# One 1 MB stage of expert weights: fetched in three pieces on earlier signals, copied inside the first swish, with the token count behind it

## The reference

```python
def hier_moe(h, w_group, b_group, w_fine, b_fine, w_gate, w_up, w_down):
    x2 = h.reshape(n_tok, d)
    g_prob = softmax(x2 @ w_group + b_group)            # 4 groups, the best one is taken
    g_val, grp = lax.top_k(g_prob, 1)
    f_logits = x2 @ w_fine + b_fine                     # 8 experts in that group, the best two
    top_v, top_i = lax.top_k(f_in_group, MOE_TOPK)
    gates = g_val * softmax(top_v)
    ...
    def expert_block(args):                             # for every expert
        xb = x2[tok]
        hid = jax.nn.silu(xb @ w_gate[e]) * (xb @ w_up[e])
        return hid @ w_down[e]
```

## Time and profile before

| | |
|---|---|
| median of 3 runs | 1109.93 us (1109.8 to 1110.1) |
| the profiled execution's own time | 1110.2 us |
| its span, first to last instruction | 1108.4 us |
| PE busy | 903.1 us (81%) |
| DVE busy | 416.5 us (38%) |
| ACT busy | 243.8 us (22%) |
| POOL busy | 41.9 us (4%) |
| moved by DMA | 440.73 MB, mean 398 GB/s |
| mean granted TensorE clock | 0.910 |

### The profile page before, as it was taken

How to read it: one execution, slowest core, us unless ns; L and a number is a source line. 1 busy time by engine, 2 the same in 40 slices (tenths; PEclk the granted TensorE clock), 3 DMA queues, 4 the chain that set the end, 5 groups by cost and what they waited for, 6 DMA issues and landing times.

```text
span 1108.4 us, 21929 instructions
## 1 busy us (share of the span) xinstructions
PE 903.1 (81%) x9146; PEld 593.1 (54%) x9146; DVE 416.5 (38%) x1006; ACT 243.8 (22%) x622; POOL 41.9 (4%) x65
## 2 busy tenths in 40 slices
PE   9999989978685867677799998999676858585875
PEld 6877745645353535353488676656443525353532
DVE  6888433332222222222288665333221222222222
ACT  5567311100000000000265863111010000000012
POOL 0012200000000000000000312000000000000000
PEclk9999989989887888788999999999887978888899
DMA  9898999999999999999998668999999999999995
GB/s 353 251 402 334 358 410 429 427 429 429 429 428 428 429 427 429 429 429 428 408 386 345 233 270 356 427 427 429 427 430 429 427 428 430 427 428 430 429 426 234
DMA packets 56577, 440.73 MB, mean 398 GB/s; under 512 B 12113, under 2 KB 12625, under 8 KB 31058
## 3 DMA queue, kind: packets, MB, share of 16 engines
q1 hardware_dynamic: 56240, 440.02, 95.7%
q10 hardware_dynamic: 290, 0.07, 0.0%
HBM read 439.03 MB, written 1.05 MB: 397 GB/s over the span
## 4 chain that ended last, share of the span: by engine, by line
PE 49%; DMA 35%; SPq 5%; another core or an unknown queue 3%; DVE 3%; ACT 2%; issue 1%; POOL 0%; POOLq 0%; ACTq 0%; DVEq 0%
DMA ring<-in_w_expert_up 27%; PE banks L1138 14%; DMA ring<-in_w_expert_down 7%; PE banks L1166 6%; PE banks L1106 6%; PE banks L1179 3%; PE banks L1015 3%; PE banks L1019 3%; PE banks L1016 3%; SPq L524 2%; SPq L472 1%; PE banks L1232 1%; PE banks L1234 1%; PE banks L1233 1%
## 5 line engine op out<-in xcount | busy, mean ns | idle before, releaser
L1138 PE MATMUL banks<-ring,scratch 128*32 128x256 f32 x4096 | 287.2, 443 | 129.2 <-DMA ring<-in_w_expert_up 128.8
L1138 PEld LDWEIGHTS banks<-ring,scratch 128*32 128x32 f32 x4096 | 150.3, 127 | 260.2 <-issue 122.2
L1665 DVE TENSOR_SCALAR scratch<-scratch 128x128 f32<-128x128 f32 x64 | 14.5, 227 | 510.3 <-ACT scratch L779 507.6
L1166 PE MATMUL banks<-ring,xn 128*32 128x256 f32 x2048 | 137.0, 410 | 7.7 <-DMA ring<-in_w_expert_down 7.5
L778 ACT ACTIVATE scratch<-banks 128x128 f32<-128x128 f32 x64 | 17.8, 278 | 511.1 <-PE banks L1138 499.7
L1106 PEld LDWEIGHTS banks<-scratch,h 128*128 128x128 f32 x448 | 107.7, 334 | 5.8 <-issue 5.8
L1106 PE MATMUL banks<-scratch,h 128*128 128x128 f32 x448 | 110.4, 405 | 0.0
L1179 PE MATMUL banks<-xn 32*128 32x256 f32 x1024 | 74.8, 403 | 36.5 <-ACT xn L788 36.5
L1166 PEld LDWEIGHTS banks<-ring,xn 128*32 128x32 f32 x2048 | 63.6, 116 | 60.0 <-issue 23.1
L1179 PEld LDWEIGHTS banks<-xn 32*128 32x128 f32 x1024 | 50.3, 186 | 67.8 <-issue 67.7
L1440 DVE SCALAR_TENSOR_TENSOR split<-ring,gains,split 128x512 fp32r<-128x512 f32 x96 | 69.7, 765 | 24.1 <-ACT split L826 23.3
(11 more groups left out here) (177 smaller groups left out, 792.9 us busy)
## 6 DMA issues: line engine op xcount, KB each, us to landing
ring<-in_w_expert_gate SPq DMA_DIRECT2D x62, 2048.0 KB, 45.5
ring<-in_w_expert_up SPq DMA_DIRECT2D x61, 2048.0 KB, 48.8
ring<-in_w_expert_down SPq DMA_DIRECT2D x56, 2048.0 KB, 47.5
ring<-in_w_in_even SPq DMA_DIRECT2D x5, 2048.0 KB, 17.8
ring<-in_w_expert_down SPq DMA_DIRECT2D x10, 1024.0 KB, 10.0
ring<-in_w_in_odd SPq DMA_DIRECT2D x5, 2048.0 KB, 19.7
ring<-in_w_expert_up SPq DMA_DIRECT2D x6, 1024.0 KB, 11.0
ring<-in_w_out_even SPq DMA_DIRECT2D x2, 2048.0 KB, 9.0
```

The lines of the kernel that those rows point to most:

```text
L1138: last = pe.matmul(psum[6][32 * j:32 * j + 32, 0:2 * P].rearrange("p (a s) -> p a s", a=2), xT[:, c, SLOTS * k:SLOTS * k + SLOTS], ring[:, ...
L1166: last = pe.matmul(psum[4][32 * q:32 * q + 32, 0:QUARTER], hidT[k][:, 32 * j:32 * j + 32], ring[:, DOWN_AT[k], D * j + QUARTER * q:D * j + ...
```

## The change

SP fetches the stage in three pieces: columns 0 to 1023 (512 KB) after `placed` has its second signal of the layer, which PE sends behind the first `gather_first`; columns 1024 to 1535 and 1536 to 2047 (256 KB each) after the first and the second signal of `gathered`. On DVE, `count_rounds` is split in two. The gate shares stay where they were. `copy_stage` moves into `hidden` of expert 0, between the swish and the transpose, and the token count follows behind that transpose; the wait for POOL's gates follows it.

```diff
+STAGE_PIECES = (1024, 1536, 2048)
...
-                sp.wait_ge(gathered[l], 2)
-                sp.dma_start(stage, gate_rows[row][:, 0:512 * FIRST_PIECES[0]]).then_inc(stage_arrived, 16)
+                for begin, end in zip((0,) + STAGE_PIECES, STAGE_PIECES):
+                    if begin == 0:
+                        sp.wait_ge(placed, (T + 1) * l + T)
+                    else:
+                        sp.wait_ge(gathered[l], STAGE_PIECES.index(end))
+                    sp.dma_start(stage[:, begin:end], gate_rows[row][:, begin:end]).then_inc(stage_arrived, 16)
...
-                pool.wait_ge(stage_arrived, 16 * (l + 1))
+                pool.wait_ge(stage_arrived, 16 * len(STAGE_PIECES) * (l + 1))
...
-            def count_rounds(l, link):
+            def choice_shares(l, link):
 
                 dve.wait_ge(gexp_done, T * (l + 1))
                 by = gv[:, 8:10]
                 link(dve.scalar_tensor_tensor(out=by, in0=gv[:, 4:6], scalar=1.0, in1=gv[:, 2:4],
                                               op0=ALU.add, op1=ALU.mult))
                 dve.reciprocal(by, by).then_inc(first_gates, 1)
+
+            def count_tokens(l, link):
 
                 dve.wait_ge(placed, (T + 1) * (l + 1))
...
-                dve.wait_ge(stage_arrived, 16 * (l + 1))
+                dve.wait_ge(stage_arrived, 16 * len(STAGE_PIECES) * (l + 1))
...
                 dve.tensor_tensor(hb, eb, gb[:, P:2 * P], ALU.mult).then_inc(hid_ready[l], 1)
+                if first:
+                    copy_stage(l)
                 dve.wait_ge(hid_ready[l], e + 1)
...
-                count_rounds(l, route_link)
-                dve.wait_ge(gate_steps, GATE_STEPS * (l + 1))
-                copy_stage(l)
+                choice_shares(l, route_link)
                 for k in range(AHEAD):
                     hidden(l, k, k, first=(k == 0), links=0)
+                    if k == 0:
+                        count_tokens(l, route_link)
+                        dve.wait_ge(gate_steps, GATE_STEPS * (l + 1))
                     gate_slots(l, k, k, k, links=SILU_LINKS)
```

## The result

The changed kernel takes 1112.18 us (median of 15 runs, 1109.99 to 1115.46) where the kernel before takes 1109.80 (1107.95 to 1111.53): a ratio of 1.0025, with a 95% interval of 1.0017 to 1.0033. It is slower by 2.4 us between the medians and by 2.8 us by the ratio. My 1111.2 us, 1.3 over the kernel before, lay on the right side with half the size, and "within 0.2%", which I took for the likeliest outcome, was missed by a little; the time lies inside the 1109.9 to 1112.4 of my own case. The profiled execution has a span of 1111.0 us, 2.6 over that of before.

What follows compares the result with a forecast made beforehand. The transfer queue was taken to bound the loops, with PE mattering where it runs short. Later pairs added 0.35 us in layer 0 and 0.95 in layer 1, together +1.3: 1111.2 us, eight-in-ten range 1108.3 to 1113.5.

Steps and rivals of the forecast that it cites:

- within 0.2%: Whole kernel: the time can't be told from no change, 1107.7 to 1112.2 us; chance 62%.
- my own case: Whole kernel: late count delays PE and the pair, 1111.2 us, own range 1109.9 to 1112.4; chance 47%.
- The stage: Transfer queue before the up half: pieces start the stage earlier, gaining 0.45 us in each layer.
- The count: DVE's opening: number of rounds signalled at 138.6 instead of 135.28 in layer 0; PE's load 1.4 us later in both layers.
- PE's load and branch: PE before the gates' turn: branch holds about 6 us, so a later load delays the restart one for one, 1.4 us.
- The rival by which the stall hides the late count: PE's branch ends at its own time, restart stays at 144.76, layer 1 keeps 0.45 us: 1109.5 us; chance 18%.
- the one by which each piece pays alone: Stage transfers: three fixed costs in series, PE restarts 4.7 us late in layer 0, about 1116.8 us; chance 3%.
- The rival by which the branch isn't held: PE restarts at 141.9 at full clock, the pair never finds the queue short: 1107.3 us; chance 11%.
- From restart to pair: PE's restart to SP's pair issue: 10.9 us in both layers, pairs 0.35 and 2.45 us later than before.
- The first rival: Restart to pair: count late and half clock long in both layers, 1113.4 us; chance 21%.
- The lower bound, 1108.8: Forecast's main case with the short way from restart to pair in both layers: -0.7 and -0.45 us.
- The queue: Transfer queue at the pair: layer 0 +0.35 us, layer 1 +0.95, together +1.3, all passed to the end.

Runs made afterwards that it cites:

- count late only: The kernel before with only the token count moved behind expert 0's swish and transpose; stage in one transfer, both copies ahead of the swish: 1115.92 us, 1.0056.
- one stage: The changed kernel with the stage fetched in a single transfer instead of three pieces; copies and count stay in their new places: 1112.87 us, 1.0028.
- count early: The changed kernel with only the token count put back ahead of expert 0's swish; pieces and the copies' new place stay: 1109.2 us, 0.999.
- POOL 256: The changed kernel with POOL's share of the stage copy cut from 768 to 256 columns, DVE's raised to 1792: 1111.07 us, 1.0018.

## Why the prediction came out as it did

- **The stage.** Right: the pieces go out as the rows are read, the up half isn't earlier, the queue is short a second time ahead of it (131 GB/s at 133). 0.45 us a layer was forecast; 0.4 and 0.25 were found in the first windows over all kernels, which is 0.65 for both; the kernels without the branch speak for 1.4 (0.9987 to 0.9974).
- **The count.** Right in layer 0: the number was to be out 6.4 us behind u and was at 6.5. In layer 1 it came at 7.2. The term held no price for POOL's copy over DVE's rows: 0.36 us in layer 0, 1.05 in layer 1. No row of before shows it from this side: there the work that meets POOL's copy is DVE's copy, and it is POOL that takes longer, 2.08 us against 1.47 here. Who is held depends on who begins: in layer 0 of the kernel before without the branch, POOL begins its copy 0.05 us ahead of DVE's and keeps its 1.47 us, and DVE's copy takes 2.10 us instead of 0.83.
- **PE's load and branch.** Right: the restart follows the load by 6.9 to 7.8 us in all 22 records (eleven executions with the branch), the branch takes 5.80 to 6.70 of them, and there is no stall without it. Inside that spread the restart needn't move by the same amount: in layer 1 it was forecast 13.3 us behind u and came at 14.5, of which the late load is 0.8 and a longer branch (6.24 us against 5.80) the rest. The rival by which the stall hides the late count fell with "count late only", the one by which each piece pays alone with "one stage". The rival by which the branch isn't held gave 1107.3 us by its working; the kernel that takes the branch away has 1108.23 before the change and 1106.46 after it.
- **From restart to pair.** The middle, 10.9 us, was taken; 11.56 and 9.80 came, 10.7 on average. The pair is issued 25.4 and 24.3 us behind u; the forecast's 157.1 and 705.1 are 24.9 and 24.2. In layer 1 that agreement is luck: a restart 1.2 us later than forecast and a way 1.1 us shorter cancel. The first rival, the long way in both layers, didn't come: the two executions of the changed kernel have 11.56 and 9.80, and 12.00 and 10.16. The lower bound, 1108.8, has a slip that changes nothing above it: with the short way in layer 1 the pair is issued at 704.05 and by the sum's own 1.7 us counts from 705.75, so that layer gives -0.1 and not -0.45.
- **The queue: the term that was too small.** The sum had +0.35 us for layer 0 and +0.95 for layer 1; by the table the queue lost 0.7 and 2.0 more. I wrote that the pair is "the first point behind it where the queue is short". With PE later it isn't. The down matrix that SP issues when expert 0's down products are through goes out 7.1 and 5.3 us ahead of the pair, at 150.77 and 700.69, and it found the queue short as well. Single microseconds of the changed kernel in layer 1:

```profile
702.00:703.00 1.00, 1.00 (x20) 0.55 (x20) 0.00 (x0) 0.00 (x0) 0.00 (x0) 1.00 0.63 188
703.00:704.00 1.00, 1.00 (x24) 0.63 (x20) 0.00 (x0) 0.00 (x0) 0.00 (x0) 1.00 0.82 328
```

Issued at 700.69, the matrix counts from 702.4 if it finds the queue dry (1.7 us, as at every dry start of before), and the queue stands at 188 GB/s there. In the traces of all fourteen executions the middle window loses nothing (0.1 us at most) where this matrix is issued up to 17.3 us behind u, 0.3 to 0.8 at 17.7, and 0.6 to 1.8 from 18.3 on; before it went out at 17.1 and 15.9, after at 18.3 and 19.0. My account took it as asked for in time because it was before. By windows it is 0.8 and 0.95 us of the 2.7.

Such losses can't simply be added, though. Where the queue is dry again at the pair, all that was asked for ahead of it has arrived, and the queue's position from there on follows from the pair's issue alone. The table bears this out. Take the column "pair" and subtract "queue's loss": in layer 1 the five executions with the pair at 24.8 us or later all give 18.8 to 19.3, though their middle windows lost anything from 0.05 to 1.80 us. So in layer 0 of the changed kernel the short down matrix adds nothing: the difference is 19.4, before it is 19.3, and the loss rose by 0.7 us because the pair went out 0.8 later behind u. My sum was short there because the way took 11.56 us and not the middle. In layer 1 a difference of 19.0 makes 5.3 us of loss for the pair at 24.3, the 1.0 more than before that I had forecast. But 6.3 were lost, and in the changed kernel's second execution 6.0 where 19.0 gives 4.9. That 1.0 us is what my sum lacked. It is of the size of the middle window's 0.92, but no run moves the down matrix by itself, so that it comes from there is argued, not shown.

So the mechanism and its order were as forecast and the direction was no luck; the hold on DVE was missed, and of the 1.4 us by which the sum was short, some 0.3 are layer 0's, by the longer way, and 1.0 are the queue's in layer 1.

## What to carry to other kernels

A value that a sequencer loads ahead of a branch has a deadline of its own, and that deadline, not the data's, decides where the value is made in another engine's order. Here the load came 3.7 us later, layers added, and from the pieces alone (0.9991) to the changed kernel (1.0025) the time grew by 3.8 us. It isn't one for one at every dose: with the load 8.6 us later it grew by 6.2 (1.0056). Where a queue runs from behind a late engine, go through every issue up to the point in question, not only the last: each has its own reserve. What is lost at an earlier one counts only if the queue isn't dry again at a later one. The versions that beat both kernels are the pieces with the count left early (0.999 or 0.9991, each with an interval that ends at 0.9999); with input that needs no further rounds, leaving the branch out of PE's code brings another 0.2% (0.9974).

## What the runs showed of the hardware

- A branch on PE over the code of further rounds holds it for 5.80 to 6.70 us while the DMA queue is full, and with PE restarting at full clock a second stop of up to 3.4 us can follow two to four us later (in layer 1 of three kernels). Work put ahead of the branch to keep the clock up can so be lost again.
- After 2.2 to 3.1 us of idling, the same kernel can restart at either clock (count early: 1.00 over the way in layer 0, 0.60 in layer 1), which moves the pair's issue by 3.8 us (8.20 against 12.03). Single executions of one kernel differ by up to 6.0 us (POOL 256, 1107.86 to 1113.86); how much of that is the clock, the runs don't show.
- GpSimd's copy of 128x768 float32 takes 1.47 us alone and 2.02 to 2.11 with DVE's copy beside it; DVE's tensor_scalar (0.23) and tensor_tensor (0.29) stretched to 1.28 and 1.26 under it, while a reciprocal that was running when POOL began kept its 0.95 and left POOL its 1.47. Where POOL began first, DVE's copy of 128x1280 took 2.10 us instead of 0.83.
